# First output projection: the products of a step ordered by kind, and low weight parts of groups 2 and 3 made on GpSimd

## The reference

```
x  = x + gate * (y @ w_out)            # first output projection, residual
x  = rmsnorm(x) * final_g              # end of the first block
h  = layer_norm(x, ln_in_g, ln_in_b)   # start of the second block
... h @ w_in_2 ...                     # its channel and row projections
```

## Time and profile before

| | us |
|---|---|
| median of three runs | 2764.65 |
| lowest and highest run | 2763.58, 2766.03 |
| span of the profiled execution | 2763.9 |
| TensorE busy | 2689.4 (97%) |
| VectorE busy | 2086.6 (75%) |
| ScalarE busy | 1069.2 (39%) |
| GpSimd busy | 477.0 (17%) |
| group 3 of the projection, from 985.6 to 1041.9 | 56.3, TensorE busy 49.5 |

### The profile page before, as it was taken

How to read it: one execution, slowest core, us unless ns; L and a number is a source line. 1 busy time by engine, 2 the same in 40 slices (tenths; PEclk the granted TensorE clock), 3 DMA queues, 4 the chain that set the end, 5 groups by cost and what they waited for, 6 DMA issues and landing times.

```text
span 2763.9 us, 33573 instructions
## 1 busy us (share of the span) xinstructions
PE 2689.4 (97%) x13192; PEld 2199.6 (80%) x13192; DVE 2086.6 (75%) x2796; ACT 1069.2 (39%) x1599; POOL 477.0 (17%) x254
## 2 busy tenths in 40 slices
PE   6999999999999999999999999999999999999998
PEld 5888888888888878778875678888887888888887
DVE  6999998873724663369998886688186988887978
ACT  5111112243413332245537751365232554555332
POOL 0000000000100002001210001354211656655000
PEclk8999999999999999999999999999999999999999
DMA  5312222224325452011101032100132222225431
GB/s 223 116 63 69 94 97 61 84 92 142 99 107 175 136 176 90 31 62 39 47 30 36 32 123 96 46 31 23 62 115 80 96 77 89 87 77 188 170 99 61
DMA packets 97710, 250.18 MB, mean 91 GB/s; under 512 B 7361, under 2 KB 34369, under 8 KB 96018
## 3 DMA queue, kind: packets, MB, share of 16 engines
q1 hardware_dynamic: 93010, 231.49, 24.4%
q10 hardware_dynamic: 4288, 15.73, 1.5%
q0 software_dynamic: 256, 0.82, 0.1%
HBM read 202.92 MB, written 45.09 MB: 90 GB/s over the span
## 4 chain that ended last, share of the span: by engine, by line
PE 80%; DVE 14%; issue 2%; ACT 1%; DMA 1%; DVEq 0%; ACTq 0%
PE pair L370 16%; PE pair L372 16%; PE pair L371 16%; PE pair L3657 7%; PE pair L3242 5%; PE pair L3244 5%; PE pair L3245 5%; DVE counted L1942 3%; PE pair L2593 2%; DVE reached L1993 1%; PE pair L2156 1%; DVE top_i L1999 1%; PE pair L1754 1%; PE pair L2172 1%; PE pair L2185 1%
## 5 line engine op out<-in xcount | busy, mean ns | idle before, releaser
L370 PE MATMUL pair<-u_hi,w_hi 128*128 128x512 f32 x768 | 302.1, 393 | 1.2 <-PEq L92 0.9
L641 DVE SCALAR_TENSOR_TENSOR conv_acc<-aT,cols,conv_acc 128x1024 f32<-128x1024 f32 x232 | 297.9, 1284 | 6.7
L371 PE MATMUL pair<-u_lo,w_hi 128*128 128x512 f32 x768 | 300.3, 391 | 0.0
L372 PE MATMUL pair<-u_hi,w_lo 128*128 128x512 f32 x768 | 300.3, 391 | 0.0
L370 PEld LDWEIGHTS pair<-u_hi,w_hi 128*128 128x128 f32 x768 | 145.2, 189 | 32.7 <-issue 2.4
L371 PEld LDWEIGHTS pair<-u_lo,w_hi 128*128 128x128 f32 x768 | 145.0, 189 | 30.6 <-issue 0.7
L372 PEld LDWEIGHTS pair<-u_hi,w_lo 128*128 128x128 f32 x768 | 145.0, 189 | 30.6
L370 PE MATMUL pair<-h_hi,ch_hi 128*128 128x512 f32 x392 | 153.8, 392 | 2.8 <-ACT ch L1824 2.6
L372 PE MATMUL pair<-h_hi,ch_lo 128*128 128x512 f32 x392 | 152.7, 389 | 0.0
L371 PE MATMUL pair<-h_lo,ch_hi 128*128 128x512 f32 x392 | 152.6, 389 | 0.0
L1014 POOL TENSOR_TENSOR yrT<-yrT,gate_c 128x1024 f32<-128x1024 f32 x8 | 18.9, 2366 | 758.1 <-ACT yrT L907 758.1
(11 more groups left out here) (510 smaller groups left out, 7105.1 us busy)
## 6 DMA issues: line engine op xcount, KB each, us to landing
wt<-in_w_ch SPq DMA_DIRECT2D x60, 512.0 KB, 3.4
wo_raw<-in_w_out SPq DMA_DIRECT2D x44, 512.0 KB, 3.6
wt<-in_w_up SPq DMA_DIRECT2D x10, 1024.0 KB, 4.9
w_raw<-in_w_up SPq DMA_DIRECT2D x10, 1024.0 KB, 4.8
g_spill<-g_stage SPq DMA_DIRECT2D x40, 256.0 KB, 2.2
ada_mod<-in_ada_mod SPq DMA_DIRECT2D x4, 2048.0 KB, 14.3
wt<-in_w_conv SPq DMA_DIRECT2D x16, 512.0 KB, 3.5
qk<-qk_st SPq DMA_DIRECT2D x8, 1024.0 KB, 6.4
```

The costliest lines, as they stand in the source:

```text
L370: nc.tensor.matmul(bank, w[0], x[0], start=(first and k == 0), stop=False)
L371: nc.tensor.matmul(bank, w[0], x[1], start=False, stop=False)
L372: return nc.tensor.matmul(bank, w[1], x[0], start=False, stop=(last and k == n_k - 1))
L641: nc.vector.scalar_tensor_tensor(dst, x, w, conv_acc[:], ALU.mult, ALU.add).then_inc(conv_step, 1)
```

## The change

It has four parts. (1) TensorE goes through a step by kind: first x_hi w_hi for all token tiles of the group, then x_lo w_hi, then x_hi w_lo; it waits for the high weights at the start of the step, and for the low weights only before the third kind. The wait for a free pair of banks stands in the first kind. (2) The low parts of blocks 16 to 43 are made by GpSimd, in a new function ahead of its channel work; VectorE keeps those of blocks 0 to 15. (3) In group 3's end, ScalarE and VectorE take the square roots and reciprocals tile by tile, and the transposes of tiles 6 and 7 move into the third channel's half tile, ahead of its last three and last two steps. (4) ScalarE evacuates a transposed tile one weight block earlier (11 instead of 12).

```diff
@@ out_lows
                 k = K_ORDER[n % NK]
-                dve.wait_ge(wo_hi_ok, n + 1)
-                nc.vector.tensor_tensor(wo_parts[1][:, n % 2, :], ...).then_inc(wo_lo_ok, 1)
                 if n < NK:
+                    dve.wait_ge(wo_hi_ok, n + 1)
+                    nc.vector.tensor_tensor(wo_parts[1][:, n % 2, :], ...).then_inc(wo_lo_ok, 1)
                     x = x_parts(k)
@@ out_tensor
-                pe.wait_ge(wo_lo_ok, s + 1)
+                pe.wait_ge(wo_hi_ok, s + 1)
                 if g == 0:
-                    pe.wait_ge(x_lo_ok, i + 1)
-                for j, t in enumerate(O_GROUPS[g]):
-                    if g and i == 0:
-                        pe.wait_ge(gate_ok, 3 * (g - 1) + j + 1)
...
-                    for h in range(2):
-                        last = products(bank_of[j][:, h, :], ...)
+                    pe.wait_ge(x_hi_ok, i + 1)
+                x_hi, x_lo = x_parts(k)
+                w_hi, w_lo = (w[:, s % 2, :] for w in wo_parts)
+                for x, w in ((x_hi, w_hi), (x_lo, w_hi), (x_hi, w_lo)):
+                    if x is x_lo and g == 0:
+                        pe.wait_ge(x_lo_ok, i + 1)
+                    if w is w_lo:
+                        pe.wait_ge(wo_lo_ok, s + 1)
+                    for j, t in enumerate(O_GROUPS[g]):
+                        if x is x_hi and w is w_hi:
+                            if g and i == 0:
+                                pe.wait_ge(gate_ok, 3 * (g - 1) + j + 1)
...
+                        for h in range(2):
+                            last = nc.tensor.matmul(...)
+                        if i == NK - 1 and w is w_lo:
+                            last.then_inc(o1_mm, 1)
...
+            for k in range(KT):
+                if k == KT - 3:
+                    transposes(TT - 2)
+                if k == KT - 2:
+                    transposes(TT - 1)
+                channel_step(pe, 2, k)
@@ out_scalar, out_vector
-                    highs(at0 + 12 + j)
+                    highs(at0 + 11 + j)
...
+                if g == 2:
+                    for j, t in enumerate(tokens):
+                        dve.wait_ge(rms_ok, 3 + j)
+                        nc.vector.reciprocal(rr1[:, j:j + 1], sd1[:, j:j + 1]).then_inc(rr_ok, 1)
+                        dve.wait_ge(rr_ok, 3 + j)
+                        normalize(j, t)
+                    for j, t in enumerate(tokens):
+                        center(j, t)
+                        dve.wait_ge(sd_ok, 3 + j)
+                        nc.vector.reciprocal(rv1[:, j:j + 1], sd2[:, j:j + 1]).then_inc(rv_ok, 1)
+                        dve.wait_ge(rv_ok, 3 + j)
+                        finish(j, t)
+                    continue
@@ new, on GpSimd ahead of mix_gpsimd
+        def out_gpsimd(pool):
+            pool.wait_ge(wo_lo_ok, NK)
+            for n in range(NK, N_SPLITS):
+                pool.wait_ge(wo_hi_ok, n + 1)
+                nc.gpsimd.tensor_tensor(wo_parts[1][:, n % 2, :], wo_raw[:, n % 2, :],
+                                        wo_parts[0][:, n % 2, :].bitcast(F32), ALU.subtract).then_inc(wo_lo_ok, 1)
```

More of the change, by code:

```diff
@@ L1367, in out_tensor @@
                     transposes(3 * (g - 1) + i - 10)
-                pe.wait_ge(wo_lo_ok, s + 1)
+                pe.wait_ge(wo_hi_ok, s + 1)
                 if g == 0:
-                    pe.wait_ge(x_lo_ok, i + 1)
-                for j, t in enumerate(O_GROUPS[g]):
-                    if g and i == 0:
-                        pe.wait_ge(gate_ok, 3 * (g - 1) + j + 1)
[L1374 to L1377, removed]
-                    for h in range(2):
[L1379 to L1383, removed]
+                    pe.wait_ge(x_hi_ok, i + 1)
[10 more added lines that the diff above has]
+                                pe.wait_ge(gate_ok, 3 * (g - 1) + j + 1)
+                            if n == 0 and j == 0:
+                                pe.wait_ge(ot_ok, KT * TT)
+                            if n == 0 and j == 1:
+                                pe.wait_ge(pw_out, KT - 1)
+                        for h in range(2):
+                            last = nc.tensor.matmul(bank_of[j][:, h, :], x[:, k % KT, t * P:(t + 1) * P],
+                                                    w[:, h * HALF:(h + 1) * HALF],
+                                                    start=(i == 0 and x is x_hi and w is w_hi),
+                                                    stop=(i == NK - 1 and w is w_lo))
+                        if i == NK - 1 and w is w_lo:
+                            last.then_inc(o1_mm, 1)
                 if i == NK - 1:
@@ L1388, in out_tensor @@
                     last.then_inc(wo_used, 1)
[L1389 to L1396, removed]
+            channel(pe, 0, 0)
+            pe.wait_ge(gate_ok, 7)
+            channel(pe, 1, 0)
+            pe.wait_ge(gate_ok, 8)
+            for k in range(KT):
[4 more added lines that the diff above has]
+                channel_step(pe, 2, k)
             pe.wait_ge(tr_ok, TT)
@@ L1518, in out_vector @@
                     for j, t in enumerate(O_GROUPS[g - 1]):
-                        out_lows(dve, NEW * g + 12 + j)
+                        out_lows(dve, NEW * g + 11 + j)
                         low_part(t)
@@ L2387, in _ @@
             ret_gpsimd(pool)
+            out_gpsimd(pool)
             mix_gpsimd(pool)
```

20 lines of the change are left out of this document (13 added, 7 removed).

## The result

The changed kernel takes 2778.69 us (median of four runs, 2777.06 to 2779.71) against 2764.76 for the kernel before (four runs, 2763.58 to 2766.03): +13.9 us, a ratio of 1.0051, 95% interval 1.0037 to 1.0064. The forecast was 2772.7 with a range of 2767 to 2778: the sign is right, the size is too small, and the time lies 0.7 us above the range. The profiled execution took 2778.02 us.

The account below looks back on a forecast made before the run. It took TensorE, 80% of the chain that ended last, as the bound; -1.0 + 3.6 + 4.5 + 0.9 + 0 = +8.0 us on 2764.65 (span 2763.9 plus 0.75) gave 2772.7, range 2767 to 2778.

Parts of the forecast that it names:

- Group 1: Order by kind inside group 1: six products cover the wait for the low part of `y`, -1.0 us.
- group 2: GpSimd's subtractions in group 2 cost nothing: a slot's round of 7.2 us fits in 8.2 for two steps.
- `ch_lo0`: At the end, `ch_lo0` stands behind block 43 on GpSimd, so TensorE waits for the first channel: +0.9 us.
- the tail: Moved transposes and square roots by tile at the end of group 3: taken as 0, range -1.5 to +1.5 us.
- That is the step that I think decides: Order by kind at group borders: late banks, two pauses of about 2 us each at border 1 to 2, +3.6 us.
- 14 x 0.227 + 0.1 = 3.3: First border: the 14 products behind the third bank wait take 3.3 us, so step 1 begins at L+9.3.
- Rival (d): Changing banks with each product lowers TensorE's granted clock: 17.5 us, 2790 with the sum; chance 2%.
- The walk: Group 3 step by step from its border: last product at about L+60.7 against L+56.2 before, +4.5 us.
- evacuating one block earlier removes the 1.6 us for `h_lo`; it is already inside the group 3 walk: Group 3: the earlier evacuation ends TensorE's 1.6 us wait for `h_lo`, with no separate term in the sum.
- the ring: Group 3: load, high part and GpSimd's low part through one slot take 7.2 us per two steps, products 5.5.
- Rival (b): Group 3's last loads take 3.6 us without stores beside them: -3.5, so +4.5 in all, 2769.2; chance 15%.
- The median is 0.75 above the span: Offset from the profiled span of 2763.9 us to the runs' median, giving 2764.65 as the starting point.

Follow-up runs that it names:

- e8b_tail: The kernel before with only the reordered roots, reciprocals and transposes at group 3's end (part 3): 2765.09 us against 2765.30.
- e1_border: The changed kernel with the first step of groups 2 and 3 and every group's last step token tile by token tile again: 2771.81 us against 2765.27 before.
- e4_fill: The changed kernel with eight extra unread products ahead of each of the three late waits for free banks: 2777.97 us against 2765.27 before.
- e7b_shift: The kernel before with only the evacuation one weight block earlier (11 instead of 12): 2771.26 us against 2765.30.
- e5b_noshift: The changed kernel with the earlier evacuation undone (12 instead of 11 again): 2777.32 us against 2765.30 before.
- e6b_store: The changed kernel with ScalarE's wait for the store of tile 5 moved behind the high parts of blocks 41 to 43: 2777.10 us against 2765.30 before.
- e10_slots: The changed kernel with a third slot for raw weight blocks from block 16 on: 2771.27 us against 2764.50 before.
- e2_order: The kernel before with only the order of products by kind, VectorE making all low parts: 2773.69 us against 2765.27.
- e11_slots_border: The changed kernel with a third raw-weight slot, border steps tile by tile and evacuation back at 12, GpSimd's low parts kept: 2762.16 us against 2764.50 before.

## Why the prediction was wrong in its size

Of the 4.7 us between the sum of 8.0 and the 12.7 of the stage, 1.6 lie at the first border and 3.4 in group 3 with its border; the other terms make up the rest within 0.3 us.

**Group 1, group 2, `ch_lo0`, the tail**: right, each within 0.3 us (the earlier trace rows against the table above), and e8b_tail shows part 3 at -0.2. For group 1 one pair of traces would not do, but the means of all traces with the old and the new order there are 1.1 apart.

**The borders.** "That is the step that I think decides" held: e1_border gives back 7.4 of 13.9. The working held too, bank by bank. What failed is "14 x 0.227 + 0.1 = 3.3": the products behind the third wait ran at half clock. With the clock kept up by e4_fill the forecast distances come out to 0.04 us. The missing terms are 1.6 us at the first border and 1.45 at the second: the prediction priced these pauses as standing time alone, and put the clock behind them at nothing. Rival (d) looked at the clock but at the wrong cause: I cleared the order of the banks with the earlier trace rows, where waits are at most 1.5 us, and never asked what my own two pauses of 2 us would do to it.

**Group 3.** The walk reached step 12 at L+46.7 against L+45.6 forecast, though it began 1.45 late. That is partly luck: two errors nearly cancel. From step 4 to step 10 (1005.16 to 1028.49) the trace has 23.3 us and the walk 21.6, since a round took 7.84 (1007.61 to 1015.45), with GpSimd's subtractions at 3.4 beside VectorE, and not 7.2; alone they took the forecast 2.40. From step 10 to step 12 it has 7.7 and the walk 9.6, since the loads there took 4.1 us (1026.64) and 4.6 (issued at 1030.23, its high part begun at 1034.82) and not 6.00. From step 12 to the last product the prediction has 15.1 us and the trace 17.4. There the step "evacuating one block earlier removes the 1.6 us for `h_lo`; it is already inside the group 3 walk" failed: I priced only what the move takes away, and did not list what else stands on ScalarE between blocks 40 and 43; the trace has a wait of 3.99 us there and half clock behind it. e7b_shift shows the move alone at +6.0 by its median and +3.1 in its faster clump. In the changed kernel less hangs on it. Undoing it gave 1.9 (e5b_noshift), because the wait for `h_lo` that it does remove came back, with 2.5 us and a clock of its own instead of the 1.6 counted; taking out the store's wait alone gave 2.1 (e6b_store), because the ring stood right behind. That the slots, and not the transfers by themselves, held the ring is shown by the third slot (e10_slots).

Rival (b) takes the two long loads back at 3.5 us where the walk had put them in at 2.4 + 1.7 = 4.1; nothing of the result hangs on that.

**The offset.** "The median is 0.75 above the span" is one execution's luck. Every later run of before lies about 1.8 above its span, and every run with GpSimd's low parts about 2.0, so the sum started from an execution that was about 1 us slow. That us is between the 12.1 of the spans and the 13.9 of the medians, with 0.7 for the changed kernel's own profiled execution and 0.2 that the spans don't show. In which stretch the slow us lay is not shown.

**The parts alone** sum to 8.4 + 5.8 + 6.0 - 0.2 = 20.0 us by the medians, and together they cost 13.9: part of the waits fall in the same places.

## What to carry to other kernels

When the order of products is turned from tile by tile to kind by kind, every tile finishes at the end: keep the first and last step of a group tile by tile, where banks are handed over. Price a forecast pause with the clock behind it (here 1.45 to 1.6 us on top of the pause), and when a step is moved up by one in a program, read every wait that it now stands behind. When two chains arrive together, undoing either tells little; add the shared resource (here a slot) and then undo the parts again.

## What the hardware showed beyond expectation

**Clock.** After waits of 1.82 and 1.88 us with two products between them, TensorE ran at 0.50 for 3.4 us; around one of 0.50 and one of 1.82 at the next border, for 3.4 us (992.6 to 996.0); after one wait of 4.0, for 3.4 us. In e1_border 3.4 us of it came with a wait of 2.65 us and again with one of 2.22, two steps later. In e2_order and e5b_noshift the pauses of the first border had 6.8 us of it (918.2 to 925.0 in the first), yet step 1 began there only 0.2 us later than in the changed kernel, since TensorE stood for part of that time anyway. In e7b_shift a wait of 3.5 us was followed by 6 us of it. Group 3 of the kernel before has waits of up to 1.5 us at 1.00, each with whole steps between.

**GpSimd and VectorE in lockstep.** Once loads are early, the two engines alternate. First VectorE without GpSimd beside it:

```profile
1011.51 1.20 DVE xo L1494
```

That was the kernel before, a VectorE operation of that kind in the chain of its trace. Now e11_slots_border:

```profile
1002.93 21.70 POOL L1744 TENSOR_TENSOR wo_lo<-wo_raw,wo_hi 128x1024 fp32r<-128x1024 f32 x7 [0.68 <-ACT wo_hi L1454]
...
1010.13 9.89 DVE L1534 SCALAR_TENSOR_TENSOR xo<-xo,small,lb_bc 128x1024 f32<-128x1024 f32 x3
...
1008.98 1.20 PE L1408 MATMUL pair<-wo_lo,yr_hi 128*128 128x512 f32 x4 [0.32 <-POOL wo_lo L1744]
1012.32 0.96 PE L1408 MATMUL pair<-wo_lo,yr_hi 128*128 128x512 f32 x3 [0.33 <-POOL wo_lo L1744]
```

VectorE's operations take 3.30 us each there and not 1.20, GpSimd's 2.40 become 3.1, and TensorE follows at 3.34 us a step. One instruction of each takes 3.34 us together, little less than the 3.60 that they take one after the other. `tmp`, which reads a bank, kept its 1.23 beside GpSimd (1036.82, inside GpSimd's 1035.03 to 1037.42). The Trainium skill (GPSIMD Engine Reference, 8. Key points) names the contention, for VectorE instructions with two SBUF inputs; these have two, and the trace agrees. Its price here is nearly the other's whole instruction.
